# Four of the six down-projection units as seven block products instead of eight

## What is computed

```python
D_FF = 2816
DN_ALPHA = (2 * DEPTH) ** 0.25      # DEPTH = 2
def swiglu(x, w1, w3, w2):
    return (jax.nn.silu(x @ w1) * (x @ w3)) @ w2
...
    for l in range(DEPTH):
        mix = hybrid_mixer(x, ...)
        x = layer_norm(DN_ALPHA * x + mix, ln1_g[l], ln1_b[l])
        x = layer_norm(DN_ALPHA * x + swiglu(x, ffn_w1[l], ffn_w3[l], ffn_w2[l]), ln2_g[l], ln2_b[l])
```

## Time and profile before

| | |
|---|---|
| runs | 2065.63, 2067.17, 2070.45 us |
| profiled execution, its own time | 2067.2 us |
| its span, first to last instruction | 2065.2 us (2.0 us lie around it) |
| mean granted TensorE clock | 0.988 |
| busy share of TensorE, VectorE, ScalarE, GpSimd | 97%, 49%, 23%, 12% |
| L662 (down products, both layers) | 352 instructions, 151.8 us busy |
| down part of layer 0 / layer 1 | 434.19 to 510.60 us / 931.43 to 1007.67 us |

### The profile page before, as it was taken

The page is one execution under the profiler, slowest core; times in us unless marked ns, Lnnn a source line. Parts: engine busy times, 40 slices in busy tenths (PEclk is TensorE's granted clock), DMA queues, the critical chain, the costliest instruction groups (busy, mean ns, idle before and its releaser), DMA issues.

```text
span 2065.2 us, 35642 instructions
## 1 busy us (share of the span) xinstructions
PE 2002.8 (97%) x14783; PEld 1379.6 (67%) x14783; DVE 1005.5 (49%) x1741; ACT 472.6 (23%) x896; POOL 249.7 (12%) x233
## 2 busy tenths in 40 slices
PE   8999999999999999999999999899997999999996
PEld 5778869964767878994445565899976444444442
DVE  2685255612469226650568846545457233323324
ACT  3165100000426301000131144432323111111111
POOL 3684000000568100000000001000000000000000
PEclk9999999999999999999999999999997999999998
DMA  8332535544533255535822234200013999999992
GB/s 250 123 123 102 204 123 165 163 169 140 185 122 123 103 204 158 170 123 187 304 82 78 86 122 164 84 3 4 3 46 124 407 413 415 422 413 413 422 414 112
DMA packets 138707, 385.52 MB, mean 187 GB/s; under 512 B 16935, under 2 KB 64399, under 8 KB 127441
## 3 DMA queue, kind: packets, MB, share of 16 engines
q1 hardware_dynamic: 138577, 383.61, 50.1%
HBM read 382.54 MB, written 1.05 MB: 186 GB/s over the span
## 4 chain that ended last, share of the span: by engine, by line
PE 91%; ACT 4%; DVE 2%; issue 2%; DMA 0%; POOL 0%; DVEq 0%; SPq 0%; ACTq 0%; POOLq 0%
PE psum L389 17%; PE psum L635 12%; PE psum L1443 10%; PE psum L3020 9%; PE psum L2188 8%; PE psum L662 7%; PE psum L3044 5%; PE psum L2953 3%; PE psum L407 3%; PE psum L600 3%; PE psum L3075 2%; PE psum L611 1%; PE psum L2604 1%; PE psum L1648 1%; ACT arena L1814 1%
## 5 line engine op out<-in xcount | busy, mean ns | idle before, releaser
L389 PE MATMUL psum<-arena,ring 128*128 128x256 f32 x1728 | 382.3, 380 | 1.0 <-ACT arena L709 1.0
L389 PEld LDWEIGHTS psum<-arena,ring 128*128 128x128 f32 x1728 | 323.9, 189 | 55.4 <-issue 8.2
L2188 PE MATMUL psum<-arena 64*64 64x64 f32 (+1 forms) x4320 | 180.8, 238 | 6.6 <-DVE arena L2413 3.5
L2188 PEld LDWEIGHTS psum<-arena 64*64 64x64 f32 x4320 | 172.6, 134 | 8.7 <-DVE arena L2413 3.6
L662 PE MATMUL psum<-ring,arena 128*128 128x512 f32 x352 | 151.8, 592 | 0.0
L635 PE MATMUL psum<-arena,ring 128*128 128x128 f32 x1280 | 149.5, 275 | 0.0
L635 PEld LDWEIGHTS psum<-arena,ring 128*128 128x128 f32 x1280 | 146.1, 192 | 0.0
L1443 PE MATMUL psum<-arena,ring 128*128 128x512 f32 (+2 forms) x432 | 142.2, 489 | 0.0
L1443 PEld LDWEIGHTS psum<-arena,ring 128*128 128x128 f32 (+1 forms) x432 | 80.6, 187 | 61.5 <-issue 55.8
L662 PEld LDWEIGHTS psum<-ring,arena 128*128 128x128 f32 x352 | 66.6, 190 | 82.3 <-issue 82.3
L635 PE MATMUL psum<-arena 128*128 128x128 f32 x960 | 113.7, 274 | 0.0
(11 more groups left out here) (437 smaller groups left out, 2795.9 us busy)
## 6 DMA issues: line engine op xcount, KB each, us to landing
ring<-in_w_in_dram SPq DMA_DIRECT2D x29, 2048.0 KB, 8.2
ring<-in_ffn_w_dram SPq DMA_DIRECT2D x46, 1024.0 KB, 6.5
arena<-in_ex_gate_dram SPq DMA_DIRECT2D x15, 2048.0 KB, 10.6
arena<-in_ex_up_dram SPq DMA_DIRECT2D x15, 2048.0 KB, 15.1
arena<-in_ex_down_dram SPq DMA_DIRECT2D x15, 2048.0 KB, 14.6
ring<-in_ex_gate_dram SPq DMA_DIRECT2D x14, 2048.0 KB, 7.7
ring<-in_ex_up_dram SPq DMA_DIRECT2D x14, 2048.0 KB, 12.2
ring<-in_ex_down_dram SPq DMA_DIRECT2D x14, 2048.0 KB, 15.8
```

Source lines behind the costliest of these rows:

```text
L389: ins = pe.matmul(bank[:, j, :], w[:, kc, c * P:(c + 1) * P], moving[:, kc, :], start=kc == 0, stop=kc == k - 1)
L2188: ins = pe.matmul(bank[r, u, :], a[r, u], b[r, u], start=i == 0, stop=i == len(terms) - 1)
```

## The change

The contributions of `w2` units 0 to 3 are computed with seven block products per unit instead of eight. For unit u the blocks are A11, A12 (token tile 0, hidden rows 0-1 and 2-3 of the unit), A21, A22 (token tile 1) and B11, B12, B21, B22 (hidden rows 0-1 or 2-3, output columns 0-511 or 512-1023). `down_by_seven(u)` does seven products of two matmuls each, 14 instead of 16. Three products go to f2(0,0), f2(0,1) and f2(1,0) alone; the products called p1, p5, p6, p7 are shared by several outputs and gather over the four units in PSUM banks of their own. Units 4 and 5 are done as before on top of the f2 banks, with f2(1,1) starting there.

On VectorE new work is added: `down_weight_sums(u)` (four operations of 128x1024, one of them in place in the ring slot), `hidden_sums(u)` (four of 128x256, one in place in `K.hT`) and `residual()`, which joins p1, p5, p6, p7 to the scaled residual while units 4 and 5 run; the f2 banks are then added without scaling. TensorE waits for `hidden_sums(u)` ahead of the third product of a unit and for `down_weight_sums(u)` ahead of the fourth. The single event `up_sums` becomes `sums`, counted in the order of `sums_order()`.

Moved are: `second_norm(0)` in VectorE's stream (now between the sums of unit 2 and those of unit 3), `second_std(act, K, 0)` (now ahead of `mid_open_scalar`, with ScalarE's copy of p1 between them), the `next` turns of layer 1 (from behind unit 3 to behind unit 4 of token tile 0), and the start of `mid_gpsimd` (now behind unit 3). The list of PSUM groups of a layer grows from 146 to 150.

```diff
@@ -95,7 +95,7 @@
     keys += [("x1T", 0), ("x1T", 1), ("f1", 0), ("f3", 0), ("x1T", 2), ("x1T", 3)]
     for c in range(1, FFN_UNITS):
         keys += [("fp", c, i) for i in range(4)]
-    keys += [("f2", tt, hf) for tt in range(TT) for hf in range(2)]
+    keys += [("p", 1), ("p", 6), ("f2", 0, 0), ("f2", 0, 1), ("p", 5), ("p", 7), ("f2", 1, 0), ("f2", 1, 1)]
     return keys + [("next", i) for i in range(2)]
 
...
+    sums=19, p1_copied=FFN_UNITS - 1, quarters=FFN_UNITS - 1, silued=FFN_UNITS - 1, hidden_up=FFN_UNITS - 1,
 )
+
+
+BY_SEVEN = 4
+
+
+def sums_order():
+
+    order = [("w13", 1), ("x", 0), ("w13", 2)]
+    for c in range(1, FFN_UNITS):
+        order += [("w13", c + 2)] if c + 2 < FFN_UNITS else [("w2", 0)] if c == FFN_UNITS - 2 else []
+        order += [("h", c - 6)] if c in (6, 7) else []
+    return order + [("w2", 1), ("h", 2), ("w2", 2), ("h", 3), ("w2", 3)]
+
+
+def turn_of_sums(key):
+    return sums_order().index(key) + 1
+
+
+assert len(sums_order()) == LAYER_EVENTS["sums"]
 
 
 def quarter(both, w, a, b):
...
             pe.wait_ge(K.landed(("w13", c)), K.landed_count(("w13", c), l))
-            pe.wait_ge(K.sem["up_sums"], K.count("up_sums", l, c + 1))
+            pe.wait_ge(K.sem["sums"], K.count("sums", l, max(turn_of_sums(("w13", c)), turn_of_sums(("x", 0)))))
...
@@ -646,29 +665,62 @@
             up_by_seven(c)
 
         banks = {(tt, hf): K.bank(("f2", tt, hf)) for tt in range(TT) for hf in range(2)}
-        for key in banks:
-            pe.wait_ge(K.empty(("f2", *key)), K.empty_count(("f2", *key), l))
+
+        def hidden_ready(kc):
+            if kc == 0:
+                pe.wait_ge(K.empty(("f3", 0)), K.drained_count(("f3", 0), l))
+            elif kc % 2 == 0:
+                pe.wait_ge(K.sem["hidden_up"], K.count("hidden_up", l, kc // 2))
+
+        def down_by_seven(u):
+
+            pe.wait_ge(K.landed(("w2", u)), K.landed_count(("w2", u), l))
+            w, sums = K.weights(("w2", u), W2_ROWS, D), K.w2_sums[:, (u + 1) % 2]
+            b = lambda i, j: w[:, 2 * i:2 * i + 2, j * BANK:(j + 1) * BANK]
+            h = lambda i, tt: K.hT[:, 4 * u + 2 * i:4 * u + 2 * i + 2, tt * P:(tt + 1) * P]
+            s1, s2, s4 = (K.h_sums[:, u % 2, i] for i in range(3))
+            products = [(("p", 1), h(0, 0), b(0, 0)), (("f2", 0, 0), h(1, 0), b(1, 0)), (("f2", 0, 1), s4, b(1, 1)),
+                        (("p", 6), s2, sums[:, 0]), (("p", 5), s1, b(0, 1)), (("p", 7), h(0, 1), sums[:, 1]),
+                        (("f2", 1, 0), h(1, 1), sums[:, 2])]
+            for n, (key, tokens, weights) in enumerate(products):
+                if n == 0:
+                    hidden_ready(4 * u)
+                elif n == 1:
+                    hidden_ready(4 * u + 2)
+                elif n == 2:
+                    pe.wait_ge(K.sem["sums"], K.count("sums", l, turn_of_sums(("h", u))))
+                elif n == 3:
+                    pe.wait_ge(K.sem["sums"], K.count("sums", l, turn_of_sums(("w2", u))))
+                if u == 0:
+                    pe.wait_ge(K.empty(key), K.empty_count(key, l))
+                for k in range(2):
+                    ins = pe.matmul(K.bank(key), tokens[:, k, :], weights[:, k, :], start=u == k == 0,
+                                    stop=key[0] == "p" and u == BY_SEVEN - 1 and k == 1)
+                if key[0] == "p" and u == BY_SEVEN - 1:
+                    ins.then_inc(K.full(key), 1)
+            ins.then_inc(K.used_up(("w2", u)), 1)
 
...
+                hidden_ready(kc)
                 for tt, hf in keys:
+                    first = (tt, hf) == (1, 1) and kc == BY_SEVEN * W2_ROWS
+                    if first:
+                        pe.wait_ge(K.empty(("f2", 1, 1)), K.empty_count(("f2", 1, 1), l))
                     ins = pe.matmul(banks[tt, hf], K.hT[:, kc, tt * P:(tt + 1) * P], w[:, i, hf * BANK:(hf + 1) * BANK],
-                                    start=kc == 0, stop=kc == FC - 1)
+                                    start=first, stop=kc == FC - 1)
                     if kc == FC - 1:
                         ins.then_inc(K.full(("f2", tt, hf)), 1)
             return ins
 
-        for u in range(W2_UNITS - 2):
-            pe.wait_ge(K.landed(("w2", u)), K.landed_count(("w2", u), l))
-            down(u, list(banks)).then_inc(K.used_up(("w2", u)), 1)
-        if l == DEPTH - 1:
+        assert BY_SEVEN == W2_UNITS - 2
+        for u in range(BY_SEVEN):
+            down_by_seven(u)
+
+        def next_turned():
             pe.wait_ge(K.sem["dma_vec"], K.count("dma_vec"))
             for i in range(2):
                 pe.wait_ge(K.empty(("next", i)), K.empty_count(("next", i), l))
@@ -677,9 +729,12 @@
             pe.transpose(bank[:, 0:P], K.crows[:, 0, :], ident)
             n = 9 * CONV_CHUNKS - P
             pe.transpose(bank[:, P:P + n], K.crows[0:n, 1, :], ident[0:n, 0:n]).then_inc(K.full(("next", 1)), 1)
+
         for u in range(W2_UNITS - 2, W2_UNITS):
             pe.wait_ge(K.landed(("w2", u)), K.landed_count(("w2", u), l))
             down(u, [(0, hf) for hf in range(2)])
+            if l == DEPTH - 1 and u == W2_UNITS - 2:
+                next_turned()
         down(W2_UNITS - 2, [(1, hf) for hf in range(2)]).then_inc(K.used_up(("w2", W2_UNITS - 2)), 1)
...
@@ -810,6 +865,9 @@
             gate = K.quarters[:, c % 2, 0, :]
             act.activation(gate, gate, ACT.Silu).then_inc(K.sem["silued"], 1)
         if l == DEPTH - 1:
+            second_std(act, K, 0)
+        drain(("p", 1), K.dve_tmp[:, 0, :])
+        if l == DEPTH - 1:
             mid_open_scalar(act, K, l)
         for tt in range(TT):
             act.wait_ge(K.sem["x2_var"], K.count("x2_var", l, tt + 1))
...
-                    dve.scalar_tensor_tensor(out=part, in0=part, scalar=DN_ALPHA, in1=K.bank((key, tt, hf)),
-                                                       op0=ALU.mult, op1=ALU.add).then_inc(K.empty((key, tt, hf)), 1)
+                    if key == "f2":
+                        tt_op(part, part, K.bank((key, tt, hf)), ALU.add).then_inc(K.empty((key, tt, hf)), 1)
+                    else:
+                        dve.scalar_tensor_tensor(out=part, in0=part, scalar=DN_ALPHA, in1=K.bank((key, tt, hf)),
+                                                 op0=ALU.mult, op1=ALU.add).then_inc(K.empty((key, tt, hf)), 1)
                     dve.wait_ge(K.empty((key, tt, hf)), K.drained_count((key, tt, hf), l))
...
 
+        def down_weight_sums(u):
+
+            dve.wait_ge(K.landed(("w2", u)), K.landed_count(("w2", u), l))
+            if u >= 2:
+                dve.wait_ge(K.used_up(("w2", u - 2)), K.free_count(("w2", u - 2), l) + 1)
+            w, sums = K.weights(("w2", u), W2_ROWS, D), K.w2_sums[:, (u + 1) % 2]
+            b11, b12, b21, b22 = (w[:, 2 * i:2 * i + 2, j * BANK:(j + 1) * BANK] for i in range(2) for j in range(2))
+            t2, t3, t4 = (sums[:, i] for i in range(3))
+            tt_op(t3, b22, b12, ALU.subtract).then_inc(link.sem, 1)
+            dve.wait_ge(link.sem, link.count())
+            tt_op(b12, b12, b11, ALU.subtract).then_inc(link.sem, 1)
+            dve.wait_ge(link.sem, link.count())
+            tt_op(t2, b22, b12, ALU.subtract).then_inc(link.sem, 1)
+            dve.wait_ge(link.sem, link.count())
+            tt_op(t4, b21, t2, ALU.subtract).then_inc(K.sem["sums"], 1)
+
+        def hidden_sums(u):
+
+            dve.wait_ge(K.sem["hidden_up"], K.count("hidden_up", l, 2 * u + 1))
+            if u == 0:
+                dve.wait_ge(K.empty(("f3", 0)), K.drained_count(("f3", 0), l))
+            if u >= 2:
+                dve.wait_ge(K.used_up(("w2", u - 2)), K.free_count(("w2", u - 2), l) + 1)
+            a11, a12, a21, a22 = (K.hT[:, 4 * u + 2 * i:4 * u + 2 * i + 2, tt * P:(tt + 1) * P] for tt in range(TT) for i in range(2))
+            s1, s2, s4 = (K.h_sums[:, u % 2, i] for i in range(3))
+            tt_op(s1, a21, a22, ALU.add).then_inc(link.sem, 1)
+            dve.wait_ge(link.sem, link.count())
+            tt_op(s2, s1, a11, ALU.subtract).then_inc(link.sem, 1)
+            dve.wait_ge(link.sem, link.count())
+            tt_op(s4, a12, s2, ALU.subtract)
+            tt_op(a21, a11, a21, ALU.subtract).then_inc(K.sem["sums"], 1)
+
+        def residual():
+
+            x = lambda tt, hf: K.x_tok[:, tt, hf * BANK:(hf + 1) * BANK]
+            scaled = lambda out, add: dve.scalar_tensor_tensor(out=out, in0=out, scalar=DN_ALPHA, in1=add, op0=ALU.mult, op1=ALU.add)
+            p1, u, v = (K.dve_tmp[:, i, :] for i in range(3))
+            dve.wait_ge(K.empty(("p", 1)), K.drained_count(("p", 1), l))
+            scaled(x(0, 0), p1)
+            dve.wait_ge(K.full(("p", 6)), K.full_count(("p", 6), l))
+            tt_op(u, p1, K.bank(("p", 6)), ALU.add).then_inc(K.empty(("p", 6)), 1)
+            dve.wait_ge(K.empty(("p", 6)), K.drained_count(("p", 6), l))
+            dve.wait_ge(K.full(("p", 5)), K.full_count(("p", 5), l))
```

(34 more changed lines are left out.)

12 lines of the change are left out of this document (4 added, 8 removed).

## The result

The change made the kernel slower. Eight runs of the changed kernel have a median of 2077.36 us (2073.17 to 2080.65), eight of the kernel before 2067.34 us (2065.63 to 2070.45). The ratio is 1.0047, with an interval of 1.0037 to 1.0057. The profiled execution took 2080.33 us (span 2078.4 us, mean granted clock 0.980).

What follows compares the result with a forecast made beforehand. TensorE, busy 97% of the span, was taken to bound the kernel. Layer 0 gains 6.87 us and layer 1 loses 14.6 (12.6 plus 2.0 for the clock): +7.7 on 2067.2 gives 2074.9 us, range 2071.5 to 2079.5.

Steps and rivals of the forecast that it cites:

- The sum: Whole kernel: -6.87 us in layer 0 and +14.6 in layer 1 make +7.7 on 2067.2, so 2074.9 us.
- Price of a matmul: Down parts: a removed matmul saves its spacing, 0.4292 us an instruction, not the 0.592 us duration; 13.73 us in all.
- Slack of units 0 to 2: Layer 0, and these units of layer 1: new sums are in time, smallest slack 4.0 us; TensorE waits nowhere.
- The rival in which VectorE is late elsewhere: Other units: sums on ring slots take twice as long, giving 2080 to 2082 us; chance 0.08, shared with the bank rival.
- the one about the banks: Seven products save nothing, as two matmuls in a row hit one bank: 2089 us; within a shared chance of 0.08.
- The stop: Unit 3 of layer 1: TensorE stands 16.2 us until VectorE has done the ctx norm and the hidden sums.
- The second stop: Unit 3 of layer 1, one product after TensorE resumes: another 3.3 us, since the weight sums need 5.0.
- that cover: Unit 3 of layer 1: the 5.0 us of weight sums cover the 3.4 us of a slow first product after resuming.
- The clock: Layer 1, after TensorE's pause in unit 3: low clock costs 2.0 us over 16 instructions; bounds nothing and 6.9.
- clock back at once: Rival: same pause in unit 3 of layer 1, but no low-clock cost afterwards; 2072.9 us, chance 0.20.
- two cases: Same pause in layer 1's unit 3: with low clock afterwards 2074.9 us, chance 0.62; without it 2072.9 us, chance 0.20.
- The range: Whole kernel: 2071.5 to 2079.5 us, taking in pauses with or without low clock, small gaps and run spread.

## Why the prediction was right

**The sum.** 2074.9 us was forecast; the two sets of runs gave 2077.36 and 2075.12 us. In the down parts -6.87 and +14.6 were forecast; the first profile has -6.84 and +14.45, the second -6.83 and +12.50. So the mechanism and its terms held. That a median lies within 0.2 us of the forecast is luck: the down parts give +7.6 and +5.7 us, while the medians moved by +10.0 and +7.0, and the difference is not in the forecast's sum.

**Price of a matmul.** 0.4292 us an instruction held. A unit of seven starts every 12.02 to 12.03 us in layer 0 (434.29, 446.32, 458.35, 470.37, 482.40), and the duration of 0.592 us would have been wrong by a third. That a removed matmul gives its spacing and not its duration is what the version without the wait shows in both layers, 6.83 us each.

**Slack of units 0 to 2.** TensorE waits nowhere. Layer 1's down part starts at 929.55 us, 1.88 earlier than in the kernel before; with the forecast shifted by that, unit 0's weight sums end at 930.1 (930.1 forecast), unit 1's at 942.8 (942.7), unit 2's at 949.3 (949.5). GpSimd, moved too, began at 999.23 us and stood idle for another 22.38 us before its next work. The rival in which VectorE is late elsewhere is out, and so is the one about the banks.

**The stop.** `ctx` came 12.17 us behind the end of unit 2 (12.08 forecast), the norm took 5.72 (5.8), the gap before the reciprocal was 0.28 as worked out from the earlier trace rows, the hidden sums 1.7, the stop 16.02 us (16.2). The runs without the wait and with an earlier `ctx` show that these terms are causes and not companions.

**The second stop.** Forecast 3.3 us "or less", measured 1.13. The term was not wrong in time: from resume to resume it was 4.91 us (5.0 forecast), but the product between them ran slowly and filled the wait. The forecast had named that cover. The run with the weight sums ahead shows it from the other side.

**The clock.** 2.0 us forecast, 1.9 in one profile and 0.1 in the other (8.78 and 6.98 for the 16 instructions, against 6.87). The rival "clock back at once" is thus no rival but the other face of the same kernel. I gave 0.62 and 0.20 to two cases that both occur, and should have forecast a mixture, some 1 us by the two profiles. The granted clock over the stop and the second resume, in the first profile:

```profile
975.00:980.00 5.00, 0.00 (x0) 0.00 (x0) 1.99 (x4) 0.00 (x0) 0.00 (x0) 0.50 1.03 405
...
985.00:992.00 7.00, 5.62 (x6) 2.00 (x7) 5.61 (x6) 0.00 (x0) 0.00 (x0) 0.50 0.41 151
992.00:994.00 2.00, 2.00 (x4) 0.91 (x3) 0.02 (x1) 0.00 (x0) 0.00 (x0) 0.54 0.00 0
994.00:1006.00 12.00, 12.00 (x30) 5.21 (x28) 4.45 (x7) 0.00 (x0) 3.80 (x10) 1.00 0.48 169
```

The level was low at the end of the stop and stayed low until 8.5 us behind the resume. The Trainium skill (TensorE: Matmul & The Clock Gate, What's actually happening) says that one kernel meets more or fewer slow matmuls from run to run; the two profiles agree. The same section of the Trainium skill puts the penalty of the ramp under 1% of a typical kernel's span and advises against fitting a count of slow matmuls. The 1.9 and 0.1 us here are under 0.1%. With the ramp left out the forecast would have been 2072.9 us, further from both medians.

**What the forecast lacked.** First, low clock in places whose code the change leaves as it was. All eleven profiles meet it at some of the same few light stretches, in varying length: layer 1's mixer takes 425.1 us without it, 426.7 with 3.4 us of it and 429.99 with 10.2 us. The forecast took the spread from three runs, 2 us either way; here the runs of the changed kernel spread over 12 us (2068.97 to 2080.62). The range was drawn for the median and held it, but for single runs it was too narrow. Its own terms add up to 2070.9 to 2079.9 us, a little more than the 2071.5 to 2079.5 that were written. Second, the join's other reader, the next turns. Their wait did not come up in the changed kernel, since everything there is late together.

**What stays open.** The version without the wait is 16.3 and 16.7 us below the kernel before in medians, where the removed matmuls give 13.7. Between it and the changed kernel lie 25.7 and 23.7 us, where layer 1's down part gives 21.3 and 19.3. The surplus is 2.6 to 3.0 us in one comparison and 4.4 in the other. A different amount of low clock elsewhere could do it, since the profiled spans move by as much with it. The granted clocks of all runs speak for a part. Within the kernel before and the version without the wait, the longer runs have the lower clock, by some 0.7 to 1.8 us for each 0.001. The mean clock is 0.9856 before and 0.9874 without the wait in the first set, 0.9853 and 0.9860 in the second. By an estimate from these numbers the clock is worth 1.3 to 3.2 us in the first set, against a surplus of 2.6 us, but only 0.5 to 1.3 us in the second, against 3.0 us. No run here fixed the clock, so the cause of the rest stays open.

## What to carry to other kernels

Before you add a producer to an in-order engine, look at the waits that already stand in its stream near that place. An idle wait of 51 us costs nothing as long as nobody needs what is behind it, and the first sums put behind it cost a stop of 16 us; moving the wait behind them turned +0.47% into -0.8%. Price a removed operation by its spacing. Price a removed wait by the time from one landmark to the next with everything inside it, since part of it may be cover for something slow.

## What the runs showed of the hardware

The low level of TensorE's clock came without any pause of TensorE: ahead of 597 us in the changed kernel's first profile it was at work all the time, on matmuls of 1 row by 512 columns and of 128x128, and eight of the latter then took 2.08 us instead of 1.16. The price of 10.2 us at the low level was 4.9 us in that stretch. At the end of a stop of 16 us the level was low in all three profiles that have one; it came back 8.5 us behind the resume in one profile, 4.1 us behind it in another of the same kernel, and 3.1 us behind it after the stop of 11.79 us.

A transfer of `ctx` issued 1.03 us behind a ring load's release took 6.91 us until VectorE used it, and 5.19 when issued 6.98 us behind it. Of 5.95 us gained at the issue, 1.7 were lost on the way.

Small loads of parameters are issued by SP some 0.35 us apart: 17 of them stood between the last ring load and `ctx` and held it for 5.95 us.
